# Thirteen feature groups of the first mixer: x's two parts in one 512-column matmul, block by block in four accumulator banks

## What is computed

```python
h = rmsnorm(x, norm_mix_g[l])
proj = h @ w_in[l]                                  # 256 x 15368
(ml_q, ml_k, ml_v, ml_o, ml_i, ml_f, sc_b, sc_c, sc_u,
 sb_q, sb_k, sb_v, g_ml, g_sc, g_sb) = jnp.split(proj, offsets, axis=-1)
h_tilde = mlstm(ml_q, ml_k * dh ** -0.5, ml_v, i_pre, f_pre)
y_ml = head_rmsnorm(sigmoid(ml_o) * h_tilde, ml_norm_g[l], ML_HEADS)
y_sc = sc_b * causal_conv3(sc_c * sc_u, conv_w[l])
y_sb = stick_breaking(sb_q * d ** -0.5, sb_k, sb_v)
merged = sigmoid(g_ml) * (y_ml @ w_ml_proj[l]) + sigmoid(g_sc) * (y_sc @ w_sc_proj[l]) \
       + sigmoid(g_sb) * (y_sb @ w_sb_proj[l])
```

## Time and profile before

| | |
|---|---|
| median of 3 runs | 933.1 us |
| the profiled execution | 933.29 us, of which the span of its instructions is 931.6 us |
| TensorE (PE) busy | 910.1 us, 98% of the span |
| VectorE (DVE) busy | 589.5 us, 63% |
| ScalarE (ACT) busy | 479.1 us, 51% |
| granted TensorE clock, mean | 0.995 of full |

### The profile page before, as it was taken

One profiled execution on the slowest core, in us unless ns is written; L12 is line 12 of the kernel. 1 busy time (PEld: TensorE's weight loads), 2 busy tenths in 40 slices (PEclk: granted clock), 3 DMA queues, 4 the chain that ended last, 5 costly groups with the idle time before them and its releaser, 6 DMA issues.

```text
span 931.6 us, 13028 instructions
## 1 busy us (share of the span) xinstructions
PE 910.1 (98%) x5411; PEld 799.3 (86%) x5411; DVE 589.5 (63%) x619; ACT 479.1 (51%) x539; POOL 44.3 (5%) x88
## 2 busy tenths in 40 slices
PE   5999999999999999999999999999999899999997
PEld 4998998789998888888988888889888798888886
DVE  5555555467887455556577745648886667777643
ACT  6333877883435433434555535446854565555441
POOL 1000111120010000000000000000000100000000
PEclk9999999999999999999999999999999899999999
DMA  7667544543355665665565555536722465555551
GB/s 256 211 220 234 180 136 136 181 137 125 102 182 180 194 207 187 193 207 198 163 200 192 181 183 192 195 111 205 253 91 91 147 211 184 182 181 203 192 169 46
DMA packets 99371, 163.95 MB, mean 176 GB/s; under 512 B 4832, under 2 KB 37315, under 8 KB 99184
## 3 DMA queue, kind: packets, MB, share of 16 engines
q1 hardware_dynamic: 99312, 163.11, 53.3%
HBM read 162.03 MB, written 3.16 MB: 177 GB/s over the span
## 4 chain that ended last, share of the span: by engine, by line
PE 93%; DVE 3%; DMA 1%; ACT 1%; issue 1%; POOL 0%; SPq 0%; DVEq 0%; ACTq 0%; POOLq 0%
PE acc L529 14%; PE acc L530 14%; PE acc L531 14%; PE acc L537 9%; PE acc L539 8%; PE acc L541 8%; PE m L562 7%; PE acc L562 5%; PE m L567 4%; PE acc L567 3%; DMA land<-in_w_in 1%; PE m L607 1%; DVE wlo L1339 1%; PE m L647 1%; PE m L634 1%
## 5 line engine op out<-in xcount | busy, mean ns | idle before, releaser
L1339 DVE TENSOR_TENSOR wlo<-land,whi 128x2048 fp32r<-128x2048 f32 (+2 forms) x153 | 337.5, 2209 | 187.6 <-ACT whi L946 187.1
L946 ACT ACTIVATE whi<-land 128x2048 fp32r<-128x2048 f32 (+2 forms) x153 | 282.0, 1848 | 212.8 <-PE acc L531 152.7
L537 PE MATMUL acc<-xT,whi 128*128 128x256 f32 x656 | 189.9, 289 | 2.0 <-DVE xT L1377 1.0
L539 PE MATMUL acc<-xT,whi 128*128 128x256 f32 x656 | 186.5, 284 | 0.0
L541 PE MATMUL acc<-xT,wlo 128*128 128x256 f32 x656 | 186.5, 284 | 0.0
L537 PEld LDWEIGHTS acc<-xT,whi 128*128 128x128 f32 x656 | 126.7, 193 | 7.0 <-issue 4.6
L539 PEld LDWEIGHTS acc<-xT,whi 128*128 128x128 f32 x656 | 126.8, 193 | 0.2
L541 PEld LDWEIGHTS acc<-xT,wlo 128*128 128x128 f32 x656 | 126.7, 193 | 0.0
L529 PE MATMUL acc<-whi,xT 128*128 128x512 f32 (+2 forms) x240 | 91.5, 381 | 0.0
L530 PE MATMUL acc<-wlo,xT 128*128 128x512 f32 (+2 forms) x240 | 90.2, 376 | 0.0
L531 PE MATMUL acc<-whi,xT 128*128 128x512 f32 (+2 forms) x240 | 90.1, 376 | 0.0
(11 more groups left out here) (385 smaller groups left out, 1303.5 us busy)
## 6 DMA issues: line engine op xcount, KB each, us to landing
land<-in_w_in SPq DMA_DIRECT2D x56, 1024.0 KB, 5.0
land<-in_w_up SPq DMA_DIRECT2D x16, 1024.0 KB, 5.1
land<-in_w_down SPq DMA_DIRECT2D x16, 1024.0 KB, 5.0
land<-in_w_ffn_gate SPq DMA_DIRECT2D x22, 512.0 KB, 3.8
land<-in_w_ffn_up SPq DMA_DIRECT2D x22, 512.0 KB, 4.8
land<-in_w_ffn_down SPq DMA_DIRECT2D x10, 1024.0 KB, 5.0
land<-in_w_out SPq DMA_DIRECT2D x6, 1024.0 KB, 5.0
land<-in_w_in SPq DMA_DIRECT2D x12, 512.0 KB, 3.9
```

The lines of the kernel that those rows point to most:

```text
L537: mm(to, whi[:, s, k, cs], xh[:, k0 + k, :], start=first and c % 2 == 0, stop=False, skip_group_check=True)
L539: mm(to, whi[:, s, k, cs], xl[:, k0 + k, :], start=False, stop=False, skip_group_check=True)
L946: activate(whi[:, u % PARTS, 0:m, 0:w], land[:, u % LANDS, 0:m, 0:w], ACT.Copy).then_inc(hi_ready, 1)
L1339: v.tensor_tensor(wlo[:, u % PARTS, 0:m, 0:w], land[:, u % LANDS, 0:m, 0:w], whi[:, u % PARTS, 0:m, 0:w].bitcast(F32), ALU.subtract).then_ ...
```

## The change

`chunked(name)` names thirteen groups: sbq1, sbk0, sbk1, mlq0, mlq1, mlk0, mlk1, scc0, scc1, scu0, scu1, scb0, scb1. They get a product of their own, `chunk_product`. Block c of 128 columns has a bank to itself: the halves of the bank hold what belongs to x's leading part and to its rest. For each block: 4 matmuls of 512 columns (whi against both parts of x), then 4 of 256 (wlo). A unit has 16 of each, where it had 48 of 256. Blocks 0 and 1 lie on side SIDE[n], blocks 2 and 3 on the other side. The side no longer alternates behind a chunked group.

DVE reads each block with one `tensor_reduce` that adds the halves: blocks 0 and 1 right after `wlo` of unit u+2, blocks 2 and 3 where the result was read before. Before it reads block 3 it waits for the whole unit. scu and scb, which multiplied out of PSUM, now multiply in SBUF behind the reads; sbq1 and mlk are scaled in SBUF.

TensorE waits: block c of a chunked group behind a chunked group, for the read of the earlier group's block c; behind another group, at block 0 for group n-2 and at block 2 for group n-1; another group behind a chunked one, for the reads of its blocks 0 and 1. `wlo` is waited for only behind the first four matmuls.

```diff
+def chunked(name):
+    return name[:3] in ("sbk", "mlq", "mlk", "scc", "scu", "scb") or name == "sbq1"
+CHUNKED = [grp[0] for grp in GROUPS if chunked(grp[0])]
+SIDE = [0]
+for _n in range(1, len(GROUPS)):
+    SIDE.append(SIDE[-1] if chunked(GROUPS[_n - 1][0]) else 1 - SIDE[-1])
...
+        def chunk_product(u):
...
+            for c in range(NG // P):
+                to, cs = acc[:, (SIDE[n] + c // 2) % 2, c % 2, :], slice(c * P, (c + 1) * P)
+                if k0 == 0 and chunked(GROUPS[n - 1][0]):
+                    pe.wait_ge(chunk_read, chunks_before(GROUPS[n - 1][0]) + c + 1)
+                elif k0 == 0 and c == 0 and n >= 2:
+                    group_read(n - 2)
+                elif k0 == 0 and c == 2:
+                    group_read(n - 1)
+                if c == 0:
+                    pe.wait_ge(hi_ready, u + 1)
+                for k in range(m):
+                    mm(to, whi[:, s, k, cs], xT[:, k0 + k].rearrange("p a t -> p (a t)"), start=k0 + k == 0, stop=False,
+                       skip_group_check=True)
+                if c == 0:
+                    pe.wait_ge(lo_ready, u + 1)
+                for k in range(m):
+                    last = mm(to[:, 0:T], wlo[:, s, k, cs], xT_hi[:, k0 + k, :], start=False, stop=k0 + k == kk - 1,
+                              skip_group_check=True)
+                if u == LAST_U[name] and c < NG // P - 1:
+                    last.then_inc(chunk_done, 1)
+            last.then_inc(units_done, 1)
...
 # in product
+            if k0 == 0 and n >= 1 and chunked(GROUPS[n - 1][0]):
+                pe.wait_ge(chunk_read, chunks_before(GROUPS[n - 1][0]) + 2)
+            elif k0 == 0 and n >= 2:
+                group_read(n - 2)
...
+        def take_chunk(name, c):
+            n, j = G_AT[name], int(name[3])
+            if c < 3:
+                dve.wait_ge(chunk_done, 3 * CHUNKED.index(name) + c + 1)
+            else:
+                product_done(name)
...
+            v.tensor_reduce(to, acc[:, (SIDE[n] + c // 2) % 2, c % 2, :].rearrange("p (a t) -> p t a", a=2), AX.X,
+                            ALU.add).then_inc(chunk_read, 1)
+        def chunks_taken(name):
+            for c in (2, 3):
+                take_chunk(name, c)
+            dve.wait_ge(chunk_read, chunks_before(name) + 4)
...
             if u != LAST_U["mix1"]:
                 split(u + 2)
+            if ends and chunked(name):
+                for c in (0, 1):
+                    take_chunk(name, c)
...
             if ends and name[:3] == "scu":
-                product_done(name)
+                chunks_taken(name)
...
-                v.tensor_tensor(zT[:, 4 * j:4 * j + 4, CONV_K - 1:], flat.rearrange("p (a b) -> p a b", b=T),
-                                cT[:, 4 * j:4 * j + 4, :], ALU.mult).then_inc(read_dve, 1)
+                z = zT[:, 4 * j:4 * j + 4, CONV_K - 1:]
+                v.tensor_tensor(z, z, cT[:, 4 * j:4 * j + 4, :], ALU.mult).then_inc(read_dve, 1)
...
             if ends and name[:3] == "scb":
-                product_done(name)
-                v.tensor_tensor(conv[:].rearrange("p a b -> p (a b)"), flat,
-                                conv[:].rearrange("p a b -> p (a b)"), ALU.mult).then_inc(read_dve, 1)
+                chunks_taken(name)
+                v.tensor_tensor(conv[:], cT[:, 4 * j:4 * j + 4, :], conv[:], ALU.mult).then_inc(read_dve, 1)
```

More of the change, by code:

```diff
@@ L141, in readers @@
 def readers(name):
-    if name[:3] == "mix" or name[:2] == "dn":
+    if name[:3] in ("mix", "sbk", "mlq", "scc") or name[:2] == "dn":
         return ()
@@ L500, in wait_operand, with group_read @@
                 turned_ready("moba0" if k1 <= 6 else "moba1", 2)
+        def group_read(n):
+            name = GROUPS[n][0]
+            if chunked(name):
+                pe.wait_ge(chunk_read, chunks_before(name) + 4)
+                return
+            for eng, seen in (("act", read_act), ("dve", read_dve)):
+                if eng in readers(name):
+                    pe.wait_ge(seen, reads_before(n, eng))
+            if name[:3] == "mix":
+                pe.wait_ge(gained, 3 + int(name[3]))
+        def chunk_product(u):
+            n, k0, m = UNITS[u]
+            name, _, _, kk, act, _ = GROUPS[n]
+            s = u % PARTS
+            wait_operand(name, act, k0 + m)
+            for c in range(NG // P):
[19 more added lines that the diff above has]
+            last.then_inc(units_done, 1)
         def product(u, between):
@@ L889, in _ @@
                 whole_product(u, between)
+            elif chunked(name):
+                chunk_product(u)
             else:
@@ L1238, in _ @@
                 product_done(f"mlo{j}")
-                activate(mlo[:, :, j * NG:(j + 1) * NG], acc[:, G_AT[f"mlo{j}"] % 2], ACT.Exp,
+                activate(mlo[:, :, j * NG:(j + 1) * NG], acc[:, SIDE[G_AT[f"mlo{j}"]]], ACT.Exp,
                          scale=-1.0).then_inc(read_act, 1)
@@ L1264, in _ @@
                 product_done(name)
-                src = banks(name)[:, :, T:] if whole(name) else acc[:, n % 2]
+                src = banks(name)[:, :, T:] if whole(name) else acc[:, SIDE[n]]
                 activate(relu[:, j % 2, :].rearrange("p (a b) -> p a b", b=T if whole(name) else NG), src,
@@ L1295, in _ @@
                 for t in range(TT):
-                    last = activate(mbv[:, t, :], acc[:, n % 2, t, :], ACT.Copy, scale=factor3[:, t:t + 1])
+                    last = activate(mbv[:, t, :], acc[:, SIDE[n], t, :], ACT.Copy, scale=factor3[:, t:t + 1])
                 last.then_inc(read_act, 1)
@@ L1383, in product_done @@
             dve.wait_ge(units_done, LAST_U[name] + 1)
+        def take_chunk(name, c):
[4 more added lines that the diff above has]
+                product_done(name)
+            k = 4 * j + c
+            to = {"sbq": sbqT, "sbk": sbkT, "mlq": mlqT, "mlk": mlkT, "scc": cT, "scu": zT, "scb": cT}[name[:3]][:, k, :]
+            if name[:3] == "scu":
+                to = to[:, CONV_K - 1:]
+            v.tensor_reduce(to, acc[:, (SIDE[n] + c // 2) % 2, c % 2, :].rearrange("p (a t) -> p t a", a=2), AX.X,
[4 more added lines that the diff above has]
+            dve.wait_ge(chunk_read, chunks_before(name) + 4)
         def sb_softplus(h):
@@ L1824, in _ @@
                 if name[:3] == "out":
-                    last = v.tensor_tensor(x, acc[:, n % 2], x, ALU.add)
+                    last = v.tensor_tensor(x, acc[:, SIDE[n]], x, ALU.add)
                 else:
@@ L1895, in _ @@
                     for t in range(TT):
[L1896 removed]
+                        last = v.tensor_scalar(to[:, t, :], acc[:, SIDE[n], t, 0:width(n)], factor3[:, t:t + 1], None,
                                                ALU.mult)
```

61 lines of the change are left out of this document (29 added, 32 removed).

## The result

The changed kernel takes 954.38 us, the median of 4 runs (952.90 to 955.53), against 933.15 for the kernel before: a ratio of 1.0226, 95% interval 1.0211 to 1.0241. It is slower by 21 us. The profiled execution is the one of 955.53 us, span 953.7; the forecast was 948.6 us, its range 943.5 to 956.

A forecast was written before the change was run, and what follows sets the result against it. TensorE, busy 98% of the span, was taken to bound the kernel: 933.3 + 14.0 (waits less matmul savings from u 28) - 0.8 (gain before u 28) + 2.1 (clock) = 948.6 us, 8 times in 10 from 943.5 to 956.

The forecast's parts named there:

- three falls or more: Rival: clock falls at three places among the late waits, 952.8 us or a little more; 8 in 100.
- Waits: u 28 to 40: TensorE stands for ACT's mlo once, then DVE's reads; 17.1 us in sum, 14.0 net taken.
- DVE has 29.6 us without a pause: Up to the read of scb1's block 1, DVE works unbroken for 29.6 us, so gsb0 at u 40 waits 5.7.
- The reduction: DVE's tensor_reduce of a block, 512 elements from PSUM: 0.69 us, 0.65 back to back.
- The rival of a slow reduction: DVE's reduction at 0.82 to 1.23 us adds 2.2 to 9.6 us: 951 to 958; 12 in 100.
- Fewer matmuls: TensorE's chunked units have 16 matmuls less, saving 0.20 us each, 5.2 us over 26 units.
- Before u 28: 14 units gain 2.8 us, less waits of 1.1, 0.45 and 0.5 at u 5, 18 and 20: net 0.8.
- I take one fall, 2.1: Behind a long TensorE wait the granted clock falls to half once, costing 2.1 us; bounds nothing to 10.
- Nothing given back: From psb0 on, DVE is needed no sooner than before, wlo of u 42 being ready, so the delay stays whole.
- DVE is not late: Rival: DVE reads every group's blocks before TensorE's demand, leaving only the matmul gain, 928.1 us; faster: 4 in 100.
- The clock holds: Rival: same TensorE waits but no fall of the clock, 946.5 us; 25 in 100.
- The change doesn't save what it says: Rival: chunked units cost what 48 small matmuls cost, 5.2 us more, 953.8 us; 4 in 100.

The follow-up runs named there:

- the waits filled: Changed kernel with 10, 17, 14 and 22 zero-weight matmuls ahead of the late operations in TensorE's four long waits: 946.91 us.
- the widths apart: Only the seven early groups chunked, sbk0's blocks 2 and 3 read before DVE's scans, each group's first unit 16 wide then 16 narrow matmuls: 930.65 us.
- DVE's work alone: Kernel before, both bank sides kept, plus two more reductions per scc, scu and scb group and one more multiplication for scu and scb: 939.34 us.
- the late groups alone: Changed kernel with only scc, scu and scb block by block, the seven earlier groups as in the kernel before: 955.09 us.
- one tap: Changed kernel with two of the short convolution's three taps left out, so its result differs: 943.59 us.

## Why the forecast was right, and what was off

The direction, the place and the cause were as forecast, and the time lies in the range, but 5.8 us (by the medians; 6.9 by the profiled execution) above the forecast. That it lies inside is in part the width of the range: what happened is the branch of three falls or more, which had 8 chances in 100, and the upper end of 956 stands 1.6 us above the median. Point by point:

- **Waits.** Forecast 2.7, 4.6, 0.3, 3.8 and 5.7, sum 17.1; in the trace, from wanted to real start, 2.6, 4.2, none for the 0.3, 3.6 and 5.5, sum 15.9, and the releasers are those named: ACT's `mlo` once, DVE's reduction three times. From u 28 to psb0 the delay without the clock is 22.0 - 7.7 = 14.3. The lists had given 14.3 too, and the 0.3 that I took off had no reason. Two of the causes were tested by taking away what stands ahead on DVE (3.8 us of gate, 3.3 of taps): each wait gave way by about that much. ACT's wait was only covered, never removed. The last wait is near its forecast because two misses cancel. "DVE has 29.6 us without a pause" was wrong: from the end of scu1's block 0 to that of scb1's block 1 the trace has 32.2 us (272.25 to 304.41, where TensorE takes them up), with the pause of 2.81. TensorE was later too, by the 2.4 us of the fall behind u 36. With the waits filled and no fall, that pause is 0.37 us and the same stretch takes 29.8 us (269.78 to 299.55).
- **The reduction.** Taken at 0.69 and 0.65 back to back; it takes 0.68, and four take 2.47. The rival of a slow reduction is out.
- **Fewer matmuls.** 0.20 a unit forecast, 0.15 measured: 26 units give 3.9 us in place of 5.2. The term was taken from `whole_product`, which has its 16 wide matmuls in one run; the new order has runs of four. The traces show 0.15 a unit and, with the widths apart, 0.20. The Trainium skill (TensorE: Matmul & The Clock Gate, section Back-to-back issue gap) gives 2.5 ns above the time of the columns for an isolated matmul; an estimate from that figure is 0.04 a unit. The traces don't agree with it, and the measurement decides.
- **Before u 28.** Forecast a net gain of 0.8, measured 1.15. The gain is smaller (14 x 0.15 = 2.1), and so are the waits: 0.7 at u 6 instead of 1.1, and none at u 18 and 20, where I had forecast 0.45 and 0.5.
- **The clock, the term that was off.** "I take one fall, 2.1." There were four in the stretch, 7.7 us, and one at 717.9, 1.3. That is 9.0 instead of 2.1 and accounts for the 6.9 us. In the earlier trace rows the clock fell behind waits of 0.3 and 2.0 us with little work between them, and each of the four waits that I forecast, 2.7 to 5.7 us, was longer than their sum. I still called 3.8 and 4.5 only "near it", left 2.7 out, and took one fall. At every one of the four pauses, from 2.4 us up, the clock fell, during the pause or up to 1.5 us behind its end. The upper bound of 10 us, which stood in the working, was the nearer end. What brought the one at 717.9 stays open: no other trace of this study has it. The other terms come out near: the delay without the clock is 0.3 above its forecast, and the gain before u 28 makes that up with 0.35.
- **Nothing given back.** psb0's delay of 20.8 us and the 1.3 at 718 make the 22.1 us by which the span grew. `wlo` of u 42 was in time.
- **The rivals.** "DVE is not late" is out for the late groups (u 28 to 41) and holds for the early ones but for 0.7 us. "The clock holds", 946.5, was run as such with the filled waits: 946.91. "Three falls", 952.8, was nearest to what happened. "The change doesn't save what it says" is true by a quarter: 0.05 of the 0.20 us a unit.

## What to carry to other kernels

Before giving up double buffering for a cheaper inner loop, list, for each group, when the engine that reads the result gets to it, and not how busy it is: here DVE was 83% busy, and the reads came 1.6 to 6 us after the next group's start, which two sides hid and one doesn't. Do the change only for the groups whose readers come in time: that took 931.3 us against 954.4, though it is at best 0.2% better than the kernel before. And price each new pause of TensorE like those here, 2.1 to 5.3 us in a dense stream, with a stretch of half clock on top, here 1.6 to 2.9 us each (1.6 with DVE's work alone, 2.9 at u 36 with the late groups alone), until a trace shows otherwise.

## What the runs showed of the hardware

- A pause of 2.07 us in a dense stream was followed by a fall of the clock (288.5, with DVE's added work), one of 1.93 (one tap) and one of 1.41 (DVE's added work) by none, each in one traced execution. At every pause of 2.4 us or more in the stretch it fell, 17 of them in five kernels. But how long the clock stayed at half varied with the same pause: 3.4 us or 6.8 behind the 5.3 us wait. Each fall that lies whole within a trace here has one of these two lengths.
- Filling the wait with matmuls on a weight of zeros kept the clock at 1.00 at all four places and shortened the stretch by 7.3 us, without making the late operations later.
- A change between a run of 512-column and a run of 256-column matmuls costs about 10 ns, an estimate from one kernel: (5.62 - 5.56) / 6, for six more of them in a unit.
- A `tensor_reduce` over pairs 256 elements apart in PSUM takes 0.68 us for its 512 input elements, as the `TENSOR_REDUCE` of 512 elements in SBUF does, 0.69.
